# Latent attention: Fourier rows turned during the spread of the rotated key, and weights placed after the next step's maximum

## The reference, cut to what matters

```python
k_c, v_c = mla_kv(ckv_a, ck_pe, kv_norm, w_kvb, None)
k_l, v_l = mla_kv(kv_a, k_pe, kv_norm, w_kvb, rope)
q_l = mla_q(q_a, q_norm, w_qb, rope)
a_l = blocked_dense_attention(q_l, concat(k_c, k_l), concat(v_c, v_l), MLA_SCALE)
y_l = concat([fourier_mix(f_in) * silu(f_gate), a_l * silu(m_gate)]) @ w_out
...
a_c = dense_attention(q_c, k_c, v_c, MLA_SCALE)
y_c = concat([fourier_mix(cf_in) * silu(cf_gate), a_c * silu(cm_gate)]) @ w_out
```

## Time and profile before

| | us |
|---|---|
| median of three executions | 1088.18 |
| the profiled execution, its own time | 1088.91 |
| its span | 1086.9 |
| PE busy | 1054.9 |
| DVE busy | 682.3 |
| ACT busy | 553.2 |
| first scores to the first product after the attention | 828.89 to 880.70 |

### The profile page before, as it was taken

One profiled execution on the slowest core, in us unless ns is written; L12 is line 12 of the kernel. 1 busy time (PEld: TensorE's weight loads), 2 busy tenths in 40 slices (PEclk: granted clock), 3 DMA queues, 4 the chain that ended last, 5 costly groups with the idle time before them and its releaser, 6 DMA issues.

```text
span 1086.9 us, 15600 instructions
## 1 busy us (share of the span) xinstructions
PE 1054.9 (97%) x5974; PEld 883.0 (81%) x5974; DVE 682.3 (63%) x1201; ACT 553.2 (51%) x1002; POOL 77.8 (7%) x95
## 2 busy tenths in 40 slices
PE   7999999999999999999999999999998999999997
PEld 6889777788887988777688778899996678889785
DVE  5986676666546786676566447523457744976664
ACT  6654365555436554365555445334426643544772
POOL 1000110000002000110000000001000002121040
PEclk9999999999999999999999999999999999999999
DMA  9644485775666744486885585233222021442001
GB/s 330 208 141 153 152 276 194 248 220 188 196 189 219 233 137 154 142 292 207 270 255 181 169 326 147 73 92 108 78 79 56 1 70 48 154 156 98 2 1 40
DMA packets 109844, 170.73 MB, mean 157 GB/s; under 512 B 7245, under 2 KB 70746, under 8 KB 109514
## 3 DMA queue, kind: packets, MB, share of 16 engines
q1 hardware_dynamic: 107668, 161.95, 46.6%
q0 software_dynamic: 1568, 6.37, 1.7%
q10 hardware_dynamic: 534, 1.41, 0.3%
HBM read 168.19 MB, written 1.05 MB: 156 GB/s over the span
## 4 chain that ended last, share of the span: by engine, by line
PE 85%; DVE 5%; ACT 3%; issue 3%; DMA 2%; SPq 0%; POOL 0%; DVEq 0%; POOLq 0%; ACTq 0%
PE PS L482 16%; PE PS L487 16%; PE PS L483 15%; PE PS L3032 4%; PE PS L3036 4%; PE PS L3033 4%; PE PS L989 2%; PE PS L1834 1%; PE PS L950 1%; PE PS L955 1%; PE PS L951 1%; PE PS L1822 1%; PE PS L1945 1%; DMA raw<-w_gate_up 1%; PE PS L999 1%
## 5 line engine op out<-in xcount | busy, mean ns | idle before, releaser
L452 DVE TENSOR_TENSOR low<-raw,high 128x1024 fp32r<-128x1024 f32 (+3 forms) x182 | 202.1, 1117 | 184.5 <-ACT high L442 183.5
L482 PE MATMUL PS<-high,hT_high 128*128 128x512 f32 (+2 forms) x796 | 303.0, 381 | 0.5 <-ACT high L442 0.5
L483 PE MATMUL PS<-high,hT_low 128*128 128x512 f32 (+2 forms) x796 | 295.7, 372 | 0.0
L442 ACT ACTIVATE high<-raw 128x1024 fp32r<-128x1024 f32 (+3 forms) x186 | 179.3, 972 | 213.3 <-PE PS L487 116.8
L487 PE MATMUL PS<-low,hT_high 128*128 128x512 f32 (+2 forms) x796 | 231.9, 372 | 1.2 <-DVE low L455 1.2
L482 PEld LDWEIGHTS PS<-high,hT_high 128*128 128x128 f32 x796 | 150.3, 189 | 34.1 <-issue 9.6
L487 PEld LDWEIGHTS PS<-low,hT_high 128*128 128x128 f32 x796 | 147.5, 188 | 23.8 <-DVE low L455 2.8
L483 PEld LDWEIGHTS PS<-high,hT_low 128*128 128x128 f32 x796 | 150.5, 189 | 19.5
L455 DVE SCALAR_TENSOR_TENSOR low<-raw,vec_cols,high 128x512 fp32r<-128x512 f32 x176 | 123.7, 747 | 67.3 <-ACT high L445 67.2
L445 ACT ACTIVATE high<-raw,vec_cols 128x512 fp32r<-128x512 f32 x176 | 117.1, 715 | 63.8 <-DMA raw<-w_gate_up 31.3
L3032 PE MATMUL PS<-high,fT_high 128*128 128x512 f32 x176 | 69.5, 395 | 0.0
(11 more groups left out here) (376 smaller groups left out, 1598.5 us busy)
## 6 DMA issues: line engine op xcount, KB each, us to landing
raw<-w_gate_up SPq DMA_DIRECT2D x176, 256.0 KB
raw<-w_mod SPq DMA_DIRECT2D x48, 512.0 KB
raw<-w_down SPq DMA_DIRECT2D x44, 512.0 KB
raw<-w_in SPq DMA_DIRECT2D x56, 384.0 KB
raw<-o_w_in SPq DMA_DIRECT2D x20, 512.0 KB
raw<-w_out SPq DMA_DIRECT2D x16, 512.0 KB
raw<-e_w_in SPq DMA_DIRECT2D x12, 512.0 KB
raw<-w_in SPq DMA_DIRECT2D x8, 512.0 KB
```

The costliest lines, as they stand in the source:

```text
L442: last = e.activation(g.high, g.raw, ACT.Copy)
L452: last = e.tensor_tensor(g.low, g.raw, g.high.bitcast(F32), ALU.subtract)
L482: e.matmul(bank, xh[:, k, tokens], g.high[:, i, :], start=first and i == 0, stop=False)
L483: e.matmul(bank, xl[:, k, tokens], g.high[:, i, :], start=False, stop=False)
```

## The change

The four Fourier units are turned by PE right after `mla_turn_pe`, each as soon as its bank has been copied out, and so ahead of the wait for `s_key`. ACT makes high parts 0, 1 and 2 before step 0 and part 3 at step 7. DVE takes the low part 2 after max(0) and part 3 after weights(6) in step 7. In DVE's loop each max(i) is followed by weights(i-1); weights(31) stands behind the loop, and so behind the low part of the third pair of heads, which ends step 31.

```diff
@@ mla_attention_pe
             pairs = len(mla_steps) // 2
-            for u in range(4):
-                ye_turn_pe(e, u)
             for p in range(pairs + 2):
@@ mla_attention_act
-            ye_high_act(e, 0)
-            ye_high_act(e, 1)
+            for u in range(3):
+                ye_high_act(e, u)
             for i in range(n + 2):
...
                 if i >= 2:
                     mla_copy(e, act, i - 2)
-                if i == 3:
-                    ye_high_act(e, 2)
+                if i == 7:
                     ye_high_act(e, 3)
@@ mla_attention_dve
                 g, r = divmod(i, 8)
-                if i % 2:
+                if i:
                     weights(i - 1)
-                    weights(i)
-                if i == 3:
-                    ye_low_dve(e, 2)
-                    ye_low_dve(e, 3)
+                if i in (0, 7):
+                    ye_low_dve(e, 2 if i == 0 else 3)
                 if g and r == 6:
                     gated_pair(g - 1)
                 if g and r == 7:
                     ya_low_dve(e, g - 1)
+            weights(n - 1)
             gated_pair(MLA_GROUPS - 1)
             ya_low_dve(e, MLA_GROUPS - 1)
@@ late_pe
             mla_turn_pe(e)
+            for u in range(4):
+                mla_taken(e, 8 + YE_UNITS[u][2])
+                ye_turn_pe(e, u)
             for n_unit in range(2 * MH - 7, 2 * MH + 1):
                 mla_taken(e, n_unit)
             e.wait_ge(s_key, 16)
```

## The result

The changed kernel took 1091.47 us in the median of 14 executions (1089.35 to 1093.16), the kernel before 1088.13 (14 executions beside them): ratio 1.0035, 95% interval 1.0028 to 1.0043. It is slower: the medians lie 3.3 us apart and the ratio is worth 3.8 us, where +2.8 was forecast; 1091.47 lies 0.5 above the forecast of 1091.0 and inside its range. The profiled execution has a span of 1091.1 us against 1086.9.

The account below looks back on a forecast made before the run. PE, busy 1054.9 of 1086.9 us, was taken as the bound. Window terms summed to +2.95, trimmed to +2.8 and added to the median of 1088.18: 1091.0 us, range 1087.9 to 1092.2.

Parts of the forecast that it names:

- Part one: Start of attention: Fourier rows turned before the key lands, so first scores at 827.15 instead of 828.89, -1.74 us.
- First group: First attention window: 11.65 us for 12.91, so -1.26, with step 1 0.77 late.
- The holds behind max: Odd steps' transposes on PE: late by 0.23, 0.40, 0.48 and 0.32 us, one of each per group.
- The unproved 0.20: DVE's 256-wide max: assumed to start 0.20 us after its scores end, as at 512; bounds 0.16 and 0.20.
- half of a bound off for 0.16: Total: eight holds 0.04 shorter would give -0.3; half of that taken off +2.95 gives +2.8.
- 0.04 shorter: The eight holds behind 256-wide scores: each would be this much shorter by the skill's constant of about 166 ns.
- The sum: All attention windows: -1.74, -1.26, +1.43, +1.50, +1.43 and tail +1.59, in all +2.95 us on a span of 1086.9.
- The long holds: Transposes behind a gated pair's low part: about 0.97 us late at steps 15 and 23, 2.1 at step 31.
- The clock: PE's clock in the attention: read as 1.00 in every window; no term for a fall.
- Free holds: Rival: weights queued behind max reach PE in time, plain holds vanish, 1085.8 us; 8 in 100.
- A high half that is early: Rival: ACT's high half of the gated pair is ready earlier, 2.9 us less, 1088.1, no change; 10 in 100.
- Turning not hidden: Rival: Fourier rows meet an uncopied bank or the key lands later, -1.74 is gone, 1092.7 us; 5 in 100.

Follow-up runs that it names:

- experiment 3: The changed kernel with weights(31) ahead of the last low part on DVE: 1089.66 us, ratio 1.0014 to the kernel before.
- experiment 5: The changed kernel with each gated pair's low part one place later on DVE, behind weights(15), (23) and (31): 1088.77 us, ratio 1.0010 to the kernel before.
- experiment 7: The changed kernel with DVE's old order of weights, but low parts ahead of weights(15), (23) and (31): 1088.44 us, ratio 1.0007 to the kernel before.
- the kernel of 2: Experiment 2: the changed kernel with DVE's old order, both weights after the odd max: 1085.22 us, ratio 0.9976 to the kernel before.
- experiment 1: The kernel before with only PE's early turning of the Fourier units; ACT and DVE as before: 1085.49 us, ratio 0.9980.
- the filled kernel: The changed kernel with 16 unread identity transposes on PE between those of steps 30 and 31: 1091.26 us, ratio 1.0033; again 1090.70 us, 1.0028.
- experiment 8: The kernel before with only DVE's new order of weights, PE and Fourier parts as there: 1096.11 us, ratio 1.0085.

## Why the prediction was right

- *Part one, -1.74.* Right: -1.82 in the profile of the change, -1.74 alone, and PE took the turned rows with no wait behind the keys. Costing the nine waits in PE's queue at nothing was right to 0.1 us: from the first turned row to the first scores are 1.86 (824.52 to 826.38) where there were 1.77.
- *First group, -1.26.* Right: -1.17.
- *The holds behind max* (a hold is the time by which weights queued behind a waiting max make the odd transposes late). Right as a mechanism and by pieces: 0.40 and 0.49 for 0.40 and 0.48. The unproved 0.20 behind 256-wide scores is shown now, as PE ends scores(15) at 849.51, so scores(14) at 849.08, and max(14) starts at 849.28. Taking half of a bound off for 0.16 was therefore a step the wrong way. The Trainium skill ("TensorE: Matmul & The Clock Gate", Single matmul latency) has its constant of about 0.17 us for a bf16 product of any width. These rows agree in that the delay is the same at both widths, at 0.20 for float32, 0.03 more than the constant. By that rule the 0.20 measured at 512 already held at 256, so the "0.04 shorter" of the forecast didn't follow from it.
- *The sum, +2.95.* Too small by 0.4 (3.36 without the clock). The terms that were mis-sized are the groups, +1.68, +1.60 and +1.52 for 1.43, 1.50 and 1.43: each hold also costs some 0.06 when PE starts again. From late transposes of 256-wide weights to the values are 0.37 us (850.22 to 850.59), where I had 0.22 + 0.09. In the second group, the four stretches of transposes are 0.38, 0.30, 0.46 and 0.55 longer than before, for holds of 0.32, 0.23, 0.40 and 0.48 forecast; that is the whole +1.68. The old trace had such a restart (861.86 to the values at 862.45), and a hold was costed as its delay alone.
- *The long holds.* Right: 2.06 late for 2.1 at step 31, and 0.84 for 0.97 at step 15 (the row below); experiments 3, 5 and 7 take them out and put them in. Had they been the whole story, experiment 5 would have equalled the kernel of 2; it is 3.26 above it, which is the plain holds.

```profile
853.43 0.38 PE L1757 MATMUL PS<-consts,z_late 128*128 128x128 f32 x2
854.49 0.44 PE L1757 MATMUL PS<-consts,z_late 128*128 128x128 f32 x2 [0.67 <-DVE z_late L1878]
```

- *The clock.* Missed. I had written that it is 1.00 in every window and didn't ask what a wait of 2 us would do to it. In an execution where it falls it costs 0.46 in the values and 1.03 in the products behind.
- *Luck.* The time came within 0.5 us although a term worth 1.49 us in the profiled execution was missing. How much of it the median holds isn't known, nor how much the slow clock costs the median of before elsewhere; so the mechanism is confirmed by the pieces in the profile, and the closeness of the total is in part chance.
- *The rivals.* Free holds: out by experiments 2 and 5. A high half that is early: out, DVE waits 1.05 for L1727. Turning not hidden: out by experiment 1.

What is open: how often the clock falls behind the last wait. It fell in both profiles of the change, in neither of the filled kernel, and not in the profiles of experiments 7 and 8, whose last wait was as long, 1.84; the two timed pairs gave 0.0002 and 0.0016 of difference in the ratio. The granted clock of all the executions, averaged for each kernel, points the same way but doesn't settle it: 0.9955 to 0.9968 in the four series with the long last wait, 0.9975 to 0.9981 in the five that turn early and have a short one, 0.9966 and 0.9977 in the two filled ones, 0.9970 to 0.9975 in the kernel before. That the idle stretch makes the clock fall is therefore likely, and not shown.

## What to carry to other kernels

On an engine that takes its instructions in order, look at what an instruction *waits for*, not only at how long it lasts: a max that waits for scores PE has just begun takes the weights queued behind it along, and 0.3 to 0.55 us per pair of steps outweighed the waits it removed. Price a reordering by the chain from the release of the first waiting instruction to the last one that PE needs, against what PE has to do meanwhile. A change made of two parts should be timed by parts: one was worth -1.7 us of attention by itself, the other cost 6.3 on top of the first and 8.7 alone, slow clock included.

## What the runs showed of the hardware

- A single stretch of 1.84 us in which PE was idle, amid work at the full clock, was followed by a granted clock of 0.50, so 1.2 GHz (883.00 to 884.50), in both profiles of the change; with 16 transposes in the wait the clock was 1.00, and in experiments 7 and 8 it stayed at 1.00 behind an equal wait. Behind the 2.67 us wait of experiment 8 it was 0.61 on the mean of 838 to 842. Behind the early wait for ACT it was 0.59 on the mean of 44 to 48 in the profile of before (a wait of 2.68) and 1.00 in that of the change (2.62). So waits of one length were followed by either clock.
- With the clock falling among them, sixteen value records took 1.59 in place of 1.13; in experiment 8, right behind the long wait, 1.91 in place of 1.02.
- A wait of PE ends with a restart: 0.05 to 0.06 us more than the delay itself (850.22 to 850.59 is 0.37 for 0.31).
- A DVE instruction that waits for scores starts 0.20 us behind their end, at 512 and at 256 columns alike (843.62 to 843.82 before, 849.08 to 849.28 after).
